# A refill of the expert-weight ring that no longer waits for the first gather, in a one-core transformer block

## What is computed

```python
h = h + merged @ w_out[l]
h = h + memory_cross_attention(rms_norm(h, cross_norm[l]), ...)
y_f = hier_moe(rms_norm(h, ffn_norm[l]).reshape(b * s, d), ...)   # 32 experts, top 2 per token
h = h + y_f.reshape(b, s, d)
return rms_norm(h, final_norm)

# inside hier_moe, for each expert e and the tokens tok that chose it:
xb = x_pad[tok]
hb = jax.nn.silu(xb @ w1[e]) * (xb @ w3[e])
(hb @ w2[e]) * gte[:, None]
```

## Time and profile before

| | |
|---|---|
| runs | 1051.43 us median of 3 (1050.07 to 1052.33) |
| the profiled execution | 1051.55 us, span 1049.8 us |
| PE busy | 997.7 us (95%) |
| DVE, ACT, POOL busy | 503.1, 343.2, 41.9 us |
| DMA | 260.72 MB, mean 248 GB/s; q1 (SP's queue) 248.08 MB |
| mean granted clock of TensorE | 0.989 |

### The profile page before, as it was taken

One profiled execution on the slowest core, in us unless ns is written; L12 is line 12 of the kernel. 1 busy time (PEld: TensorE's weight loads), 2 busy tenths in 40 slices (PEclk: granted clock), 3 DMA queues, 4 the chain that ended last, 5 costly groups with the idle time before them and its releaser, 6 DMA issues.

```text
span 1049.8 us, 12592 instructions
## 1 busy us (share of the span) xinstructions
PE 997.7 (95%) x4901; PEld 629.3 (60%) x4901; DVE 503.1 (48%) x915; ACT 343.2 (33%) x684; POOL 41.9 (4%) x59
## 2 busy tenths in 40 slices
PE   8999999999999999999997999999999889898894
PEld 7778867766778889877786344444343333333342
DVE  5369799765466445532336333333332232333236
ACT  6442365667763245443232211111111110111113
POOL 1000000000000000000000100000000000000001
PEclk9999999999999999999997999999999999999998
DMA  8422312112113626322278999999999999999992
GB/s 238 130 81 81 120 41 81 41 42 80 41 45 117 234 87 198 123 81 86 73 327 312 381 429 426 427 427 426 426 426 425 429 425 429 425 428 426 426 406 90
DMA packets 64431, 260.72 MB, mean 248 GB/s; under 512 B 11329, under 2 KB 39026, under 8 KB 50802
## 3 DMA queue, kind: packets, MB, share of 16 engines
q1 hardware_dynamic: 59954, 248.08, 59.6%
q0 software_dynamic: 3104, 7.35, 1.9%
q10 hardware_dynamic: 1312, 4.46, 1.2%
HBM read 259.60 MB, written 4.19 MB: 251 GB/s over the span
## 4 chain that ended last, share of the span: by engine, by line
PE 75%; DMA 13%; DVE 6%; issue 3%; ACT 1%; SPq 0%; DVEq 0%; POOLq 0%
PE ps L1958 16%; DMA eraw<-in_w 12%; PE ps L1649 12%; PE ps L1650 12%; PE ps L1651 12%; PE ps L2011 8%; PE ps L2022 2%; PE ps L2023 2%; PE ps L1884 1%; PE ps L1906 1%; PE ps L1826 1%; PE ps L1834 1%; DVE s L1273 1%; DVE nmax L1275 1%; PE ps L1852 1%
## 5 line engine op out<-in xcount | busy, mean ns | idle before, releaser
L1958 PE MATMUL ps<-eraw,XT 128*64 128x512 f32 x992 | 225.9, 598 | 12.8 <-DMA eraw<-in_w 11.6
L1224 DVE TENSOR_TENSOR wlo<-raw,whi 128x2048 fp32r<-128x2048 f32 (+2 forms) x43 | 95.9, 2230 | 115.6 <-ACT whi L906 115.5
L1958 PEld LDWEIGHTS ps<-eraw,XT 128*64 128x64 f32 x992 | 67.4, 136 | 133.7 <-issue 129.5
L2011 PE MATMUL ps<-eraw,HT 128*64 128x512 f32 x512 | 113.0, 593 | 8.2 <-issue 8.2
L1518 DVE TENSOR_TENSOR h<-ps,h 128x512 f32<-128x512 f32 x128 | 79.4, 684 | 82.8 <-PE ps L2023 82.8
L1649 PE MATMUL ps<-xT_hi,whi 128*128 128x512 f32 (+1 forms) x256 | 104.0, 406 | 1.6 <-DVE xT_lo L1231 1.6
L1650 PE MATMUL ps<-xT_lo,whi 128*128 128x512 f32 (+1 forms) x256 | 100.0, 391 | 0.0
L1651 PE MATMUL ps<-xT_hi,wlo 128*128 128x512 f32 (+1 forms) x256 | 100.0, 390 | 0.0
L906 ACT ACTIVATE whi<-raw 128x2048 fp32r<-128x2048 f32 (+2 forms) x43 | 80.1, 1864 | 45.5 <-PE ps L1651 45.3
L2011 PEld LDWEIGHTS ps<-eraw,HT 128*64 128x64 f32 x512 | 39.4, 137 | 79.9 <-issue 79.9
L1064 ACT ACTIVATE HT<-ps 128x512 f32<-128x512 f32 x15 | 9.0, 598 | 197.7 <-PE ps L1996 197.7
(11 more groups left out here) (316 smaller groups left out, 1577.4 us busy)
## 6 DMA issues: line engine op xcount, KB each, us to landing
eraw<-in_w SPq DMA_DIRECT2D x82, 2048.0 KB, 29.1
eraw<-in_w SPq DMA_DIRECT2D x28, 1024.0 KB, 10.8
raw<-in_w_in SPq DMA_DIRECT2D x9, 1024.0 KB, 5.2
raw<-in_w_gate SPq DMA_DIRECT2D x8, 1024.0 KB, 5.4
raw<-in_w_ckv SPq DMA_DIRECT2D x8, 1024.0 KB, 5.3
raw<-in_w_out SPq DMA_DIRECT2D x4, 1024.0 KB, 5.2
raw<-in_w_cq SPq DMA_DIRECT2D x4, 1024.0 KB, 5.1
raw<-in_w_co SPq DMA_DIRECT2D x4, 1024.0 KB, 5.0
```

The lines of the kernel that those rows point to most:

```text
L1224: dve.tensor_tensor(wlo[n % 2][:, 0:w], raw[n % RING][:, 0:w], whi[n % 2][:, 0:w].bitcast(f32), ALU.subtract).then_inc(w_lo, 1)
L1958: ins = pe.matmul(ps[1 + c // 2][rows, :], XT[p % 2][:, kk, rows], eraw[slot][:, first + 512 * k:first + 512 * k + 512], start=(kk == 0), ...
L2011: ins = pe.matmul(ps[4 + n][rows, :], HT[:, ff, rows], eraw[slot][:, first + D * f + 512 * n:first + D * f + 512 * n + 512], start=(ff == ...
```

## The change

```diff
@@ -707,7 +707,6 @@
                 load_place(n)
 
             sp.wait_ge(xf_stored, 16 * TT)
-            sp.wait_ge(blk_loaded, 16)
             load_place(NS - 1)
             for n in range(2 * NS, len(LOADS)):
                 sp.wait_ge(e_wused, LOADS[n][-1])
```

## The result

The changed kernel takes 1057.07 us (median of 6 runs, 1055.02 to 1058.20) where the kernel before, measured beside it, takes 1051.16 (6 runs, 1048.98 to 1052.33). The ratio is 1.0052, with a 95% interval from 1.0040 to 1.0064: slower by 5.9 us, where 1.5 us were forecast and the range ended at 1055.6. The direction was right; the loss is four times the one that was forecast. The profiled execution lies low among its six: 1055.53 us, span 1053.8 us, 4.0 us more than the span before. So the profile shows less than the median's loss, and that turns out to matter.

A forecast was written before the change was run, and what follows sets the result against it. The prediction took the start of the saturated weight stream as the bound. Gather +1.7 and stream -0.2 made +1.5 us on the profiled 1051.55, 1053.05, forecast as 1052.9 us against the runs' median; range 1050.8 to 1055.6.

The forecast's parts named there:

- What bounds the kernel: Expert part, from about 595 us: SP's weight stream is saturated, so a later start of it ends the kernel equally later.
- Place 8 moves directly behind place 7, and gains nothing: Weight stream before fill 9: place 8 lands at 578.0, gaining only 0.2 us (between 0 and 0.3).
- The gather's lateness: Pair 0's gather, issued at 573.78 into a stream running until 578.0, lands 1.7 us later (bounds 0 to 2.4).
- The model row: Gather of pair 1, issued at 580.1 while place 8 moved, took 5.0 us; used to size pair 0's delay.
- rule of turns between queues: DMA engines alternate between queues a packet at a time; for pair 0's gather this gave +1.1 us, time 1052.3.
- The clock: Rival, chance 0.25: PE's clock falls in the longer pause before the first weight matmuls, giving 1054.3 us.
- The clock's price: First weight matmuls: 2.7 us at half rate lose about 1.4 us, up to 2.5 if the transposes fall in it.
- earlier stream: Rival, chance 0.06: place 8's early load brings fill 11 and all behind it forward, -3.2 us, giving 1048.2 us.
- absence of delay: Rival, chance 0.10: gather finds its turn at once, or place 8 still comes late: 1051.2 to 1051.4 us.
- gather of 10 us: Rival, chance 0.06: pair 0's gather is starved as in the steady stream, +7.2 us, giving 1058.4 us.

The follow-up runs named there:

- b_half_full: Kernel before with only place 8's first half loaded ahead of the gather wait, 12 idle matmuls ahead of pair 0's transposes and 2 behind: 1052.25 us, ratio 1.0009.
- b_place8_late: Kernel before with place 8's load waiting for the first use of place 0, as fill 9 does: 1056.65 us, ratio 1.0045.
- a_awake15: Changed kernel with 15 idle matmuls in place of 9 ahead of pair 0's transposes: 1056.49 us, ratio 1.0044.
- a_small: Changed kernel with place 8 loaded by eight DMAs of 256 KB, rows of 2 KB and not 8 KB: 1057.84 us, ratio 1.0053.
- b_late: Kernel before with three more clears of blk on POOL ahead of pair 0's gather, no load beside it: 1059.06 us, ratio 1.0071.
- b_late_awake15: Kernel before with three more clears ahead of pair 0's gather and 15 idle matmuls in place of 9: 1058.63 us, ratio 1.0064.
- b_half_early: Kernel before with only place 8's first half loaded ahead of the wait for the gather: 1054.10 us, ratio 1.0029.
- a_full: Changed kernel with 18 idle matmuls in place of 9 ahead of pair 0's transposes and 2 behind them: 1055.55 us, ratio 1.0036.
- b_late_full: Kernel before with three more clears ahead of pair 0's gather, 18 idle matmuls ahead of the transposes and 2 behind: 1054.36 us, ratio 1.0032.
- a_again: Changed kernel run again unaltered, for a second profile: 1057.61 us, ratio 1.0051.
- b_full: Kernel before with 10 idle matmuls in place of 9 ahead of pair 0's transposes and 2 behind them: 1051.38 us, ratio 0.9995.

## Why the prediction was wrong, step by step

- **What bounds the kernel: right.** "When the saturated stream begins" was the thing to ask. From the end of the second group of transposes to the end of the span it is 459.5 us before and 459.0 and 459.5 in the two profiles of the changed kernel; all the others lie within 458.9 to 459.8, but for b_half_full at 460.5, for which no cause was looked for. In b_place8_late, where the stream itself starts with more in it, it is 463.5.
- **Place 8 moves directly behind place 7, and gains nothing: right in kind.** Forecast -0.2 us, measured 0 to -0.5, which cannot be told from nothing (above). Its landing at 578.0 was a wrong number: it landed at 579.6. The 4.9 us counted bytes at 427 GB/s from place 7's landing, while the last pieces of place 8 moved one by one until 579.2, when most of it was through by 578 (the transfers by queue, above).
- **The gather's lateness: right mechanism, too small.** Forecast 1.7, bounds 0 to 2.4; measured 2.66 and 2.74, outside of the bounds. The model row, the gather of pair 1, had its load's last landing at 584.6 and itself landed at 585.1, 0.5 us behind it. That was the rule to read from it, though one row could not show that it holds. The forecast took the 5.0 us of it as a latency instead, and compared how long before the stream's end it was issued. With landing = load ahead + 0.5, even the wrong 578.0 gives a landing of 578.5 and 1.4; with the right 579.6 it gives 580.1 as measured. So the term that failed is place 8's landing. From the Trainium skill's rule of turns between queues ("DMA: Bandwidth & Descriptors", "Queues, rings and completion order") the prediction worked out 1.1 us. It took a turn to be one row; the page has a turn last for a whole packet, typically some 9 to 17 descriptors, so the 1.1 us is not what the page's rule gives. The two queues do share the engines in a_awake15 (0.22 MB beside 0.88 MB), so turns as such are not against the traces; but the gather landed no earlier for them, at 579.8, and with rows of 2 KB in the load (a_small) no earlier than with 8 KB.
- **The clock: put at nothing in the sum, and it fell.** The sum is +1.7 - 0.2, with no term for the clock; the fall stood as a rival with a chance of 0.25. It fell in both profiles of the changed kernel, and in each of five other profiles with PE quiet longer than before (a_awake15, b_late, b_late_awake15, b_half_early, a_small), in b_half_early with 3.6 us from the end of the idle matmuls to the first weight matmul, where before it was 3.0. It held in the three in which idle matmuls filled most of the pause (a_full, b_late_full, and b_half_full, where 1.4 us of idle time were left ahead of the transposes and 0.4 behind them). The argument against it, that PE waits up to 1.7 us beside transposes in the expert part and keeps its clock, had one pause of 1.7 us in mind; here there are two pauses, 3.3 and 1.2 us, around 1.1 us of transposes. Its other row, the fall at 558.1, was of another kind: PE was busy for 3.10 of the 3.10 us before it, with the router's narrow matmuls.
- **The clock's price: too small.** Forecast 1.4, up to 2.5; measured 1.48 in one profile and 3.68 in the other. The 2.7 us of the rise at 571 was taken as the duration of the low clock. It was down from some point in 578 to 580 until some point in 588 to 590 in a_again, transposes and all; in the changed kernel's first profile for some 3.4 us (an estimate from its stretches of 1 us).
- **The other rivals** are out. No earlier stream (b_half_full gains nothing), no absence of delay, and no gather of 10 us.

So two steps of the prediction failed. The gather's term of 1.7 us was mis-sized, since place 8 was put at 578.0 and landed at 579.6; it measured 2.7. And the clock, which the sum put at nothing, took 1.5 to 3.7 us. The range ended at 1055.6, which left the two together 4.2 us; in a_again they came to 6.4.

## To carry to other kernels

In this kernel a load that was let go early beside a small transfer on the critical path made that transfer land behind the last of what was queued ahead of it. So take the landing of the last load ahead, not the bytes, and do it before asking what the early load gains. Ask next what PE does in the longer pause: in front of the dense work a delay of 0.9 us cost 1.4 us more at 1.2 GHz (b_half_early), and one of 2.7 us cost 1.5 to 3.7 us more. And look for where a stream waits for its consumer: a load in that gap was free here, and moving it earlier could not pay, as the next fill hangs on the consumer's progress. When two profiles are compared, compare them from the same step on: here up to 2.7 us of a difference lay ahead of anything that was edited.

## What was not expected of the hardware

- The gather landed 0.2 to 0.6 us behind the load queued ahead of it in seven profiles, with rows of 8 KB in that load and, in one of them, of 2 KB. What sets both landings in the changed kernel are the last few pieces, which move one by one when all else is through: three rows out of 55 decide when the gather has landed.
- One and the same kernel loses 1.48 or 3.68 us to the clock, by when in the pause the fall comes. A single profile can understate the median, as here.
- Behind three clears of the same buffer, POOL's indirect DMA took 2.1 us and not 1.08, in all three kernels that had them. What lengthens it stays open.
- The runs of the kernel before lie up to 4.5 us apart, too (1048.85 to 1053.39 in 21 runs), and the clock has a part in it at other places. In the profiles of b_full, b_half_full and b_late_full the 48 router matmuls ahead of the experts take 5.28 us in the chain; in the kernel before, where the clock falls at 558.1 and so beneath them, they take 7.19. And in the profiles of a_full, b_late, b_late_awake15 and b_place8_late there is one more fall, at 229 us; in these four the router's matmuls start at 556.5 to 557.1, in the other ten at 554.9 to 555.8. That these two are all of the spread was not shown. In b_place8_late the mean clock from 229 to 234 us is 0.66, where it is 1.00 in the kernel before, and the router's matmuls start at 556.75. Here is the chain's row for b_full:

```profile
555.80 5.28 PE ps L1917 x48
```
